# Hybrid decoder layer on one core: the first head's queries and eight experts ahead of the rest

## What is computed

```python
q = (hf @ w_q).reshape(tokens, PEER_HEADS, 2, PEER_HALF)
s1 = jnp.einsum('thd,hnd->thn', q[:, :, 0], keys1)
s2 = jnp.einsum('thd,hnd->thn', q[:, :, 1], keys2)
v1, i1 = lax.top_k(s1, 16); v2, i2 = lax.top_k(s2, 16)
cand_score = v1[..., :, None] + v2[..., None, :]        # 16 x 16 for each token and head
top_score, pos = lax.top_k(cand_score, 16)              # with expert_id = i1 * 128 + i2
act = gelu(einsum('tkd,td->tk', u_tab[expert_id], hf))
y = einsum('tk,tkd->td', softmax(top_score) * act, v_tab[expert_id])
```

## Time and profile before

| | |
|---|---|
| executions shown | 1653.38 to 1654.88 us, median 1653.81 |
| profiled execution: span, first to last instruction | 1657.0 us |
| PE / DVE / ACT / POOL busy | 82% / 64% / 21% / 47% of the span |
| granted TensorE clock, mean | 0.914 of 2.4 GHz |
| moved by DMA | 599.35 MB, 362 GB/s over the span |
| first gather of U issued | 243.75 us |

### The profile page before, as it was taken

The page is one execution under the profiler, slowest core; times in us unless marked ns, Lnnn a source line. Parts: engine busy times, 40 slices in busy tenths (PEclk is TensorE's granted clock), DMA queues, the critical chain, the costliest instruction groups (busy, mean ns, idle before and its releaser), DMA issues.

```text
span 1657.0 us, 16021 instructions
## 1 busy us (share of the span) xinstructions
PE 1355.5 (82%) x5078; PEld 669.4 (40%) x5078; DVE 1063.8 (64%) x2871; ACT 348.9 (21%) x776; POOL 775.5 (47%) x848
## 2 busy tenths in 40 slices
PE   8999899888788978877769876678877778788777
PEld 7866574432455644642213320122332333333323
DVE  4625249957777889976555766444565666666656
ACT  2321422211342322011002120021122222222221
POOL 3000005766676657775467777355433333334332
PEclk9999999999998989997779997689999998998999
DMA  4223807999999999999999999999999999999995
GB/s 154 77 102 115 299 25 269 380 411 412 409 409 409 411 396 409 408 409 411 398 411 409 409 410 411 418 412 417 420 422 422 421 421 422 422 421 422 421 422 224
DMA packets 130212, 599.35 MB, mean 362 GB/s; under 512 B 15824, under 2 KB 15824, under 8 KB 97360
## 3 DMA queue, kind: packets, MB, share of 16 engines
q0 software_dynamic: 115776, 536.92, 80.3%
q1 hardware_dynamic: 14208, 61.15, 9.6%
q10 hardware_dynamic: 144, 0.26, 0.0%
HBM read 596.18 MB, written 2.10 MB: 361 GB/s over the span
## 4 chain that ended last, share of the span: by engine, by line
DMA 44%; PE 27%; DVE 12%; POOL 8%; issue 6%; ACT 2%; DVEq 1%; ACTq 0%; SPq 0%; POOLq 0%
DMA arena<-in_peer_uv,arena 21%; DMA arena<-in_peer_v,arena 14%; DMA arena<-in_peer_u,arena 9%; PE psum L1152 7%; DVE arena L1906 5%; POOL arena L752 4%; POOL arena L740 4%; PE psum L1130 4%; PE psum L1083 3%; PE psum L816 3%; PE psum L827 3%; PE psum L1064 2%; DVE arena L1537 1%; ACT arena L1428 1%; PE psum L838 1%
## 5 line engine op out<-in xcount | busy, mean ns | idle before, releaser
L1906 DVE CUSTOM_DVE_ANT_0 arena<-arena,psum 128x1024 f32<-128x1024 f32 x512 | 622.9, 1218 | 417.7 <-DMA arena<-in_peer_uv,arena 245.8
L1152 PE MATMUL psum<-arena 128*128 128x512 f32 x880 | 426.5, 642 | 98.3 <-ACT arena L1428 98.3
L740 POOL DMA_INDIRECT arena<-in_peer_u,arena x288 | 272.4, 946 | 363.4 <-PE psum L893 226.0
L1130 PE MATMUL psum<-arena 128*32 128x512 f32 x1152 | 278.5, 726 | 128.6 <-DMA arena<-in_peer_v,arena 128.5
L772 POOL DMA_INDIRECT arena<-in_peer_uv,arena x220 | 207.1, 941 | 335.2 <-PE psum L1152 299.1
L752 POOL DMA_INDIRECT arena<-in_peer_v,arena x288 | 271.5, 943 | 147.1 <-issue 76.8
L1152 PEld LDWEIGHTS psum<-arena 128*128 128x128 f32 x880 | 176.1, 205 | 352.6 <-issue 217.7
L1130 PEld LDWEIGHTS psum<-arena 128*32 128x32 f32 x1152 | 47.3, 120 | 313.9 <-DMA arena<-in_peer_v,arena 224.1
L816 PE MATMUL psum<-arena 128*128 128x512 f32 x256 | 118.5, 609 | 2.5 <-DVE st L1579 2.4
L1083 PE MATMUL psum<-arena 128*128 128x512 f32 x224 | 98.7, 593 | 1.4 <-ACT arena L1355 1.4
L827 PE MATMUL psum<-arena 128*128 128x256 f32 x384 | 93.0, 402 | 8.3 <-ACT arena L1211 7.0
(11 more groups left out here) (271 smaller groups left out, 1395.0 us busy)
## 6 DMA issues: line engine op xcount, KB each, us to landing
arena<-in_w_in SPq DMA_DIRECT2D x28, 1024.0 KB, 7.8
arena<-in_w_out SPq DMA_DIRECT2D x16, 512.0 KB, 7.9
arena<-in_peer_w_q SPq DMA_DIRECT2D x16, 512.0 KB, 14.0
arena<-in_peer_w_q SPq DMA_DIRECT2D x8, 1024.0 KB, 13.2
arena<-in_peer_u,arena POOLq DMA_INDIRECT x292, 15.5
arena<-in_peer_v,arena POOLq DMA_INDIRECT x292, 15.9
arena<-in_peer_uv,arena POOLq DMA_INDIRECT x220, 27.3
arena<-in_x SPq DMA_DIRECT2D x4, 512.0 KB, 5.1
```

What stands on the lines that cost most here:

```text
L740: pool.indirect_dma_start(row, None, u_d, bass.IndirectOffsetOnAxis(ap=eid[i % 2][:, c:c + 1], axis=0)).then_inc(landed, 16)
L1130: mm = pe.matmul(bank[6 + half][group * UK:(group + 1) * UK], zrows[k % 2][:, z0:z0 + ZW], row[:, half * 512:(half + 1) * 512], start=Fals ...
L1152: mm = pe.matmul(bank[y_bank[i][half]], diag_w[q % 2][:, j], row[:, D + half * 512:D + (half + 1) * 512], start=False, stop=c == SEL - 1 o ...
L1906: dve.tensor_tensor_reduce(row, row, h2p[i], 1.0, 0.0, ALU.mult, ALU.add, dots[:, c:c + 1]).then_inc(s["u_free"], 1)
```

## The change

Six things. The queries and scores of the first two heads are made by head: `q1(0, 0)` and `s1(0, 0)` for head 0, then, behind two attention products and a suffix sum, `q1(0, 1)` and `s1(0, 1)` for head 1. VectorE's choice for head 0 becomes `choose_first`: it finds the best 8 of 16 from the best eight keys on each side, writes their numbers and signals `eight`, and then finds the other eight. GpSimd's first gather waits for `eight` and for the state product of tile 1. `FIRST` becomes 10: the first four rows go to the memory at 80, 84, 8 and 12 KB; the last two are the places of x of tiles 2 and 3, whose load moves on SyncE behind `u_free` of 4, that is behind row 3. "on" of tile 1 is held on VectorE until row 3, and "st" of tile 1 until row 0. `load_h2(0)` moves behind the scores of head 1. The numbers that depend on `FIRST` follow.

```diff
-            ("os", 1, 0), ("st", 1, 0), ("h2T", 0, 0), ("h2T", 0, 1), ("r", 1, 1), ("sp", 1, 2), ("z", 1, 3), ("q", 0, 0),
-            ("sp", 1, 3), ("s", 0, 0), ("choose", 0, 0), ("o", 1, 0), ("o", 1, 1), ("r", 1, 2), ("o", 1, 2),
-            ("r", 1, 3), ("o", 1, 3), ("osn", 1, 0), ("on", 1, 0)]
+            ("os", 1, 0), ("st", 1, 0), ("h2T", 0, 0), ("h2T", 0, 1), ("r", 1, 1), ("sp", 1, 2), ("z", 1, 3), ("q1", 0, 0),
+            ("sp", 1, 3), ("s1", 0, 0), ("choose", 0, 0), ("o", 1, 0), ("o", 1, 1), ("r", 1, 2), ("q1", 0, 1), ("o", 1, 2),
+            ("r", 1, 3), ("s1", 0, 1), ("o", 1, 3), ("osn", 1, 0), ("on", 1, 0)]
     out += [("q", 0, 1), ("s", 0, 1), ("mix", 1, 0), ("mix", 1, 1), ("wo", 1, 0), ("wo", 1, 1), ("add", 1, 0), ("add", 1, 1),
             ("n2", 1, 0), ("xsq", 1, 0), ("q", 0, 2)]
...
-HELD = {("st", 1, 0): 1, ("add", 1, 0): 8, ("add", 1, 1): 8, ("n2", 1, 0): 8}
+ON_AT = 3
+HELD = {("st", 1, 0): 0, ("on", 1, 0): ON_AT, ("add", 1, 0): 8, ("add", 1, 1): 8, ("n2", 1, 0): 8}
...
-    if t == 0 and (kind == "h2T" or kind in ("q", "s") and i == 0):
-
-        return [(a, b)[i if kind == "h2T" else "qs".index(kind)]]
+    if kind in ("q1", "s1"):
+        return [(a, b)["qs".index(kind[0])]]
+    if t == 0 and kind == "h2T":
+        return [(a, b)[i]]
...
-        FIRST = 8
-        first_row = [at(k, D) for k in (122, 126, 174, 80, 84, 170, 178, 182)]
+        FIRST = 10
+        first_row = [at(k, D) for k in (80, 84, 8, 12, 174, 122, 126, 170, 178, 182)]
...
-            return u_row[n % UB], u_in[n % UB], (n - FIRST) // UB + 1
+            return u_row[(n - FIRST) % UB], u_in[(n - FIRST) % UB], (n - FIRST) // UB + 1
...
-            for t in range(GT, NT):
-                sp.dma_start(xs[:, t], x_d[:, t]).then_inc(x_in[t], 16)
...
+            sp.wait_ge(s["u_free"], 4)
+            for t in range(GT, NT):
+                sp.dma_start(xs[:, t], x_d[:, t]).then_inc(x_in[t], 16)
...
-                if c % TOPK == 0:
+                if n == 8:
+                    pool.wait_ge(*linked(0, 0, 11))
+                elif n and c % TOPK == 0:
                     pool.wait_ge(*linked(i, c // TOPK, 11))
 
                 if n == 0:
+                    pool.wait_ge(s["eight"], 1)
+                    pool.wait_ge(*filled("st", 1))
+                elif n == 4:
+                    pool.wait_ge(*filled("z", 1, SBH // AT_ONCE[1] - 1))
+                elif n == 5:
                     pool.wait_ge(*filled("o", 1, SBH // AT_ONCE[1] - 1))
-                elif n == 3:
-                    pool.wait_ge(*filled("st", 1))
-                elif n == 5:
+                elif n == 7:
                     pool.wait_ge(s["on_rdy"], 2)
-                elif n == 6:
+                elif n == 8:
                     for half in range(2):
                         pool.wait_ge(*filled("mix", 1, half))
                 elif FIRST <= n < FIRST + UB - 1:
...
-                    pool.wait_ge(s["u_free"], PAIRS - UB + 2 * (n - PAIRS - 9) + 2)
+                    pool.wait_ge(s["u_free"], 1 + max(m for m in range(PAIRS) if (m - FIRST) % UB // 2 == n - PAIRS - 9))
...
+                elif kind == "q1":
+                    ps = claim("q1", 0, i)
+                    if i == 0:
+                        for a in range(2):
+                            pe.wait_ge(*read("h2T", 0, a))
+                        pe.wait_ge(s["wq_in"], 16 * DC)
+                    for j in range(2 * i, 2 * i + 2):
+                        for c in range(DC):
+                            mm = pe.matmul(ps[:, j * P:(j + 1) * P], w_q_h[0][c][:, j * HALF:(j + 1) * HALF], h2T[0][:, c],
+                                           start=c == 0, stop=c == DC - 1)
+                    mm.then_inc(filled("q1", 0, i)[0], 1)
+                elif kind == "s1":
+                    ps = claim("s1", 0, i)
+                    pe.wait_ge(*read("q1", 0, i))
+                    pe.wait_ge(s["keys_in"], 16)
+                    for j in range(2 * i, 2 * i + 2):
+                        mm = pe.matmul(ps[:, j * NKEYS:(j + 1) * NKEYS], qs[0][:, j], keysT[:, j], start=True, stop=True)
+                    mm.then_inc(filled("s1", 0, i)[0], 1)
...
-                        act.wait_ge(s["u_free"], 2)
+                        act.wait_ge(s["u_free"], 7)
                     act.copy(qs[t % 2][:, 4 * i:4 * i + 4], heads(bank_for("q", t, i))).then_inc(read("q", t, i)[0], 1)
+                elif kind in ("q1", "s1"):
+                    act.wait_ge(*filled(kind, 0, i))
+                    two = slice(2 * i, 2 * i + 2)
+                    act.copy(qs[0][:, two], heads(bank_for(kind, 0, i))[:, two]).then_inc(read(kind, 0, i)[0], 1)
+                    if kind == "s1" and i:
+                        load_h2(0)
                 elif kind == "qt":
                     act.wait_ge(*filled("qt", t, i))
                     act.copy(qs[t % 2][:, 4 * i:4 * i + 4], heads(bank_for("qt", t, i))).then_inc(read("qt", t, i)[0], 1)
                 elif kind == "s":
                     act.wait_ge(*filled("s", t, i))
                     act.copy(qs[t % 2][:, 4 * i:4 * i + 4], heads(bank_for("s", t, i))).then_inc(read("s", t, i)[0], 1)
-                    if t == 0 and i == 0:
-                        load_h2(0)
...
-                    for link in range(LINKS):
-                        choose(0, 0, link)
+                    choose_first()
...
+                if link == 0 and t == 0 and h < 2:
+                    dve.wait_ge(*read("s1", 0, h))
+                elif link == 0:
...
+            def choose_first():
+
+                scores = [qs[0][:, a] for a in range(2)]
+                pair_, pair_rest = crest[:, 0:64], crest[:, 64:128]
+                first = slice(0, 8)
+                dve.wait_ge(*read("s1", 0, 0))
+                for a in range(2):
+                    dve.max(top[:, a, first], scores[a])
+                dve.drain()
+                for a in range(2):
+                    dve.max_index(topi[:, a, first], top[:, a, first], scores[a])
+                dve.tensor_tensor(pair_.rearrange("p (a b) -> p a b", a=8), top[:, 0, first].unsqueeze(2).to_broadcast([P, 8, 8]),
+                                  top[:, 1, first].unsqueeze(1).to_broadcast([P, 8, 8]), ALU.add)
+                dve.drain()
+                dve.max(best[:, first], pair_)
+                dve.drain()
+                dve.max_index(pos[:, first], best[:, first], pair_)
+                dve.tensor_tensor(code[:, :, first], topi[:, :, first], iota[:, first].unsqueeze(1).to_broadcast([P, 2, 8]), ALU.bitwise_or)
+                dve.drain()
+                dve.tensor_scalar(posk[:, 0, first], pos[:, first], 3, KEY_BITS, ALU.logical_shift_right, ALU.logical_shift_left)
+                dve.tensor_scalar(posk[:, 1, first], pos[:, first], 7, KEY_BITS, ALU.bitwise_and, ALU.logical_shift_left)
+                dve.drain()
+                few = differ.rearrange("p a m n -> p (a m n)")[:, 0:128].rearrange("p (a m n) -> p a m n", a=2, m=8)
+                for a in range(2):
+                    dve.tensor_tensor(few[:, a], posk[:, a, first].unsqueeze(2).to_broadcast([P, 8, 8]),
+                                      code[:, a, first].unsqueeze(1).to_broadcast([P, 8, 8]), ALU.bitwise_xor)
+                dve.drain()
+                dve.tensor_reduce(ids[:, 0:16], few.rearrange("p a m n -> p (a m) n"), AX.X, ALU.min)
+                dve.drain()
+                dve.scalar_tensor_tensor(eid[0][:, first], ids[:, 0:8], float(NKEYS), ids[:, 8:16], ALU.mult, ALU.add
+                                         ).then_inc(s["eight"], 1)
...
+                dve.match_replace(pair_rest, best[:, first], pair_, LOWEST)
+                for a in range(2):
+                    dve.match_replace(rest[:, a], top[:, a, first], scores[a], LOWEST)
+                dve.drain()
+                for a in range(2):
+                    dve.max(top[:, a, last], rest[:, a])
+                dve.drain()
+                dve.tensor_tensor(cand.rearrange("p (a b) -> p a b", a=TOPK), top[:, 0].unsqueeze(2).to_broadcast([P, TOPK, TOPK]),
+                                  top[:, 1].unsqueeze(1).to_broadcast([P, TOPK, TOPK]), ALU.add)
+                for a in range(2):
+                    dve.max_index(topi[:, a, last], top[:, a, last], rest[:, a])
+                dve.drain()
+                dve.tensor_copy(cand.rearrange("p (a b) -> p a b", a=TOPK)[:, first, first], pair_rest.rearrange("p (a b) -> p a b", a=8))
+                dve.drain()
+                dve.max(best[:, last], cand)
...
+                dve.scalar_tensor_tensor(eid[0][:, last], ids[:, 0:8], float(NKEYS), ids[:, 8:16], ALU.mult, ALU.add
+                                         ).then_inc(s["linked"], LINKS)
```

19 lines of the change are left out of this document (17 added, 2 removed).

## The result

| | before | changed |
|---|---|---|
| median of 17 executions each, us | 1657.49 (1653.38 to 1661.39) | 1662.37 (1658.89 to 1667.31) |
| ratio | 1 | 1.0039, interval 1.0029 to 1.0050 |
| profiled execution: span, us | 1657.0 | 1664.6 |

The change makes the kernel slower by 0.39%, 6.5 us (4.8 to 8.3); the two medians lie 4.9 us apart, at the lower end of that interval. The forecast said slower, by 5.4 us, and its 1659.2 lies 3.2 us under the median measured.

What follows compares the result with a forecast made beforehand. From about 300 us the DMA engines are full, so the end follows VectorE's row 9. Norm moved 2.8, transposes 0.5 and product's clock 2.1 sum to 5.4 us, giving 1659.2; range 1651 to 1662.5 (8 in 10).

Steps and rivals of the forecast that it cites:

- the 0.5: TensorE's two mix transposes ahead of tile 1's output product: 0.5 us more at the lower clock.
- The term that I set at 2.8: Norm of tile 1 behind row 3 makes the output product late for VectorE; row 9 comes 2.8 us later.
- the clock term: TensorE's clock falls after a 5 us hole: output product 2.1 us longer, the two transposes ahead 0.5.
- the last line of the sum: 5.4 us on the 1657.0 span gives 1662.4, 3.2 above the median of runs 1653.81, carried over: 1659.2.
- The lent rows and the x load: Two more lent rows for GpSimd's gathers, and x of tiles 2 and 3 loaded later: 0 each.
- The late squares: ScalarE's squares wait for row 9, next TensorE queries about 9 us later; put at 0, uncovered some 1.5 us.
- The fourth rival: TensorE's lag reaches the V ring, or its clock falls again before the next queries: 1.5 to 3 us more; chance 0.09.
- The clock did not hold: Rival one: TensorE's clock holds at tile 1's output product, leaving +2.8 us, 1656.6; chance 0.20.
- The earlier start was not kept: Rival two: VectorE's choice starts 4.5 us earlier and the end moves as much, 1649.3, or 2.5 us, 1651.3; chance 0.20.
- my condition: For the earlier start to be kept, VectorE's norm of tile 1 must end at 250.9 or before, 5.7 us earlier than forecast.
- Nothing was made up later: Rival three: slack between 300 and 1600 us makes up the delay, 1653.8; chance 0.05.

Runs made afterwards that it cites:

- e3: The changed kernel with six 128x512 matmuls, results overwritten, added on TensorE between the second scores and tile 1's mix transposes; 1662.01 us, 1.0025 of the kernel before.
- e4: The changed kernel with eight lent rows instead of ten and x loaded early as before; 1660.77 us, 1.0027 of the kernel before.
- e7: The changed kernel with twelve 128x512 matmuls, results overwritten, added on TensorE ahead of the transposes of tile 1's h2; 1666.28 us, 1.0064 of the kernel before.
- e1: The changed kernel with the norm of tile 1 behind row 0 instead of row 3; 1652.64 us, 0.9976 of the kernel before.
- e11: The same kernel as e1, run again on another chip; 0.9985 of the kernel before.
- e9: e1 with ScalarE's copy of h2 moved into ScalarE's own idle gap and the second scores in another PSUM bank; 1652.50 us, 0.9982 of the kernel before.
- e10: e9 with eight lent rows instead of ten and x loaded early as before; 0.9996 of the kernel before.
- e5: e1 with ScalarE's copy of h2 behind the first scores and the second scores in another PSUM bank; 1.0007 of the kernel before.
- e8: e5 with eight lent rows instead of ten and x loaded early as before; 1.0008 of the kernel before.
- e2: The changed kernel with the norm of tile 1 behind row 6 instead of row 3; 1668.07 us, 1.0065 of the kernel before.

## Why the prediction was right, and where it failed

**The mechanism and its size were right.** From q0, where both profiles can be compared (1.07 us are taken off the times of the changed kernel):

| | forecast | measured |
|---|---|---|
| choice starts | 229.4 | 229.4 |
| first gather | 232.7 | 233.1 |
| row 0 | 240.8 | 240.5 |
| norm starts, ends | 250.1, 256.65 | 250.4, 256.9 |
| product starts | 258.9 (with the 0.5) | 259.6 |
| product longer by | 2.1 | 1.65 |
| additions start | 274.55 (271.95 + 2.6) | 274.4 |
| row 9 | 281.3 | 281.4 |
| difference at row 9, us | 5.4 | 5.5 |

The eight took 3.4 us, not 3.0, and the row's use did not care, since it waits for the copy of h2, as forecast. The term that I set at 2.8 (norm moved, clock apart) is 2.9 in e3, the clock 2.6 for a forecast of 2.6. Inside the clock term the parts were off in opposite directions: the product lost 1.65 us (15.62 less 13.97) for my 2.1, and the two transposes with the copies between them 0.98 for my 0.5 (the product starts at 258.62 in e3 and 259.60 in the changed kernel, both counted from q0 of before). That they cancel is luck.

**The step that failed is the last line of the sum**: "that is 3.2 above the median of the runs, 1653.81, and the difference is taken over: **1659.2**". The difference was right; what it was added to was not. Over 17 executions the kernel before has a median of 1657.49, not 1653.81. That is 3.7 us; the difference of the two medians, 4.9 for 5.4, takes 0.5 of it back, and what remains is the 3.2 by which the forecast is low.

The runs show why three executions were a poor level. The 17 fall into two bunches, seven at 1653.4 to 1655.8 and ten at 1657.0 to 1661.4, and all three shown at first are of the lower one. There was a sign in plain sight, and I read it too small: a span is not a timed execution. In every execution on record the time is 1.7 to 3.0 us more than the span, so the profiled one of 1657.0 would have been timed at some 1659, about 5 us over my level and not 3.2. The range allowed nothing for that. Its upper end, 1662.5, was worked out from the terms alone, and the median measured lies 0.1 us inside it: that it does is luck.

**The terms that I put at nothing.** The lent rows and the x load: right, nothing up to the first V row (e4). The late squares: "the second of these queries gates the first V row ... at 302.5; GpSimd arrives at 304". The order was right, the margin was not: TensorE's side is ready at 304.0 and GpSimd issues at 304.1, with the 1.07 us taken off, so 0.13 us remained instead of 1.5. The step missed the 1.77 us that the second fall of the clock added to the queries at 287.74. One more of those would have been paid at once, as e7 shows at three times the size. The fourth rival did not come true up to the V row; whether the up to 2 us by which e4 and the changed kernel differ belong to it stays open.

**The rivals.** The clock did not hold (0.88, 0.50, 0.60 in the three stretches). The earlier start was not kept; e1 shows that 2.4 of the 4.5 us are kept at row 9 once the norm is behind row 0, and my condition, an end of the norm at 250.9 or before, fits: in e1 it ends at 250.5. Nothing was made up later: the first V row at +5.5, the last gather at +5.3.

**What the page said.** The Trainium skill, "TensorE: Matmul & The Clock Gate", section "What's actually happening", holds the warm-up ramp for under 1% of a typical kernel span. Here the clock costs 2.6 us of 1657, 0.16%, so the sentence holds; and that is nearly half of the 5.5 us that row 9 lost, so it was worth its term.

## What to carry to other kernels

A step moved on one engine is to be followed to the engine that waits for it: here 9.6 us won for the first gather were paid for by a norm that stood between TensorE and its largest product. Where TensorE is left idle for some microseconds just before long work, price that work at the lower clock as well, and look whether a small thing, a copy of 1.1 us in the wrong gap, makes such a hole. And before a difference of 0.3% is set on a level, ask how far the executions of the unchanged kernel lie apart.

## What the runs showed of the hardware that I had not expected

**The start of an execution varies by some 5 us, with the clock in its first 45 us.** With the same steps of TensorE ahead of them, the first queries began at 222.8 to 225.0 us in nine of the fourteen profiles and at 218.7 to 220.5 in five. The stage table of e11 and then of e9, two of one chip, has the difference in 20 to 60 us. Of e11:

```profile
20.00:40.00 20.00, 20.00 (x86) 17.54 (x86) 8.64 (x31) 7.50 (x16) 0.00 (x0) 0.83 0.29 106
40.00:60.00 20.00, 20.00 (x112) 18.08 (x111) 12.84 (x45) 9.76 (x21) 0.00 (x0) 0.91 0.30 106
```

Of e9:

```profile
20.00:40.00 20.00, 20.00 (x107) 17.97 (x106) 11.20 (x39) 9.15 (x18) 0.00 (x0) 1.00 0.36 120
40.00:60.00 20.00, 18.68 (x110) 16.79 (x111) 12.20 (x42) 12.57 (x26) 0.00 (x0) 1.00 0.24 92
```

In all nine late ones the clock in 20 to 40 us was 0.83, in the five early ones 0.91 or 1.00. The matmuls tell the same: the 80 of 128x256 that begin at 22.59 us in e11 and at 20.24 in e9 take 19.96 and 17.51 us, and at their end e11 is already 4.8 of its 5.5 us late. Of those 5.5 us, 3.5 are in the spans (1650.7 and 1654.2). The difference is of the size of the scatter between executions of one kernel (1650.8 to 1658.6 for e11), and the profiled executions fit: the eight late ones with a time of their own lie 0.1 to 5.2 us above the median of their kernel; of the early ones four lie between 0.7 below and 0.3 above it, and e10 3.7 below. So I take it for the main part of the scatter, and the lower bunch of the kernel before for the early kind. That is argued, not shown: only one execution of each kernel has a profile. Nor is it shown that chance decides which kind a profile is: e5, e8, e9 and e10, the four kernels with the other PSUM bank, are all early, and of the ten others only e7 is. Against the bank as the whole cause stand e7 and the timed runs of e10, which range from 1651.7 to 1659.1 like those of the rest.

**A wait that was 0.7 us longer had the lower clock behind it, in both kernels that had it.** In e5 the wait of 1.03 us instead of 0.35 had behind it four groups of 9.85 us in all (1.97, 2.02, 1.06 and 4.80), which take 6.51 in e9 (1.10, 1.08, 0.60 and 3.73); in e8 the same wait had 8.28 behind it. **But equal waits do not always end alike.** Ahead of the queries of tile 1 TensorE was idle for 2.63 or 2.64 us in five kernels: the queries then took 8.80, 8.49 and 8.75 us in the changed kernel, e3 and e5, and 7.11 in e2 and e9, where the clock did not fall. In e1 and e11 a wait of 2.90 us was followed by 9.43 and 9.38.

**The same indirect gather, issued back to back, goes out every 1.24 us** (305.21, then 306.45 in the changed kernel), and a row of 0.52 MB takes 1.27 us at the 413 GB/s of the dense stage. For rows of 4 KB, GpSimd's issue and the DMA engines are matched within 3%, so neither has room to make up a delay there. For the rows of 8 KB GpSimd has room (in the changed kernel it waits some 300 us in all for TensorE's use of them, L1176), but the DMA engines have none: from 1300 to 1500 us their share is 1.01, at 421 GB/s.
